# A four-stage recurrence pipeline: sums over channels as two float32r passes, and a new order of the steps

## The reference, cut to what matters

```
kk = k * k_k
kk = kk / max(sqrt(sum(kk * kk, over the 64 channels of a head)), 1e-12)
k  = k * (1 + (a - 1) * k_a)
S_t = S_{t-1} (diag(w_t) - kk_t^T (kk_t * a_t)) + v_t^T k_t ;  o_t = S_t r_t
mean = mean(o, over 64 channels);  var = mean((o - mean)^2, over 64 channels)
o = (o - mean) * rsqrt(var + 64e-5) * lnx_g + lnx_b
o = o + sum(r * k * r_k, over 64 channels) * v
o = (o * silu(g)) @ w_o
```

## Time and profile before

| | |
|---|---|
| median of three runs | 2069.64 us (2065.68 to 2069.98) |
| the profiled execution, own time | 2070.53 us |
| its span (first to last instruction) | 2068.7 us |
| mean granted TensorE clock | 0.971 of full speed |
| busy, share of the span | TensorE 92%, VectorE 49%, ScalarE 39%, GpSimd 12% |
| the recurrence in that span | about 498 to 922.5 us |

### The profile page before, as it was taken

The page is one execution under the profiler, slowest core; times in us unless marked ns, Lnnn a source line. Parts: engine busy times, 40 slices in busy tenths (PEclk is TensorE's granted clock), DMA queues, the critical chain, the costliest instruction groups (busy, mean ns, idle before and its releaser), DMA issues.

```text
span 2068.7 us, 49295 instructions
## 1 busy us (share of the span) xinstructions
PE 1906.9 (92%) x20670; PEld 1626.5 (79%) x20670; DVE 1015.3 (49%) x1655; ACT 811.9 (39%) x1422; POOL 248.7 (12%) x313
## 2 busy tenths in 40 slices
PE   7999999999999999999999989999999997787796
PEld 6988999999888888879897767777767675333696
DVE  6644364544455556524554633434454443577334
ACT  4233232334555555523333322323234443455232
POOL 0200000000343444313100000000000000000033
PEclk9999999999999999989999999999999998889898
DMA  7435555553222332124479999999999999999441
GB/s 278 170 133 181 167 173 167 168 176 127 72 86 87 97 93 70 46 77 163 146 282 353 418 419 398 425 425 425 425 413 416 424 421 370 391 378 409 158 154 61
DMA packets 128717, 508.93 MB, mean 246 GB/s; under 512 B 20257, under 2 KB 61602, under 8 KB 83234
## 3 DMA queue, kind: packets, MB, share of 16 engines
q1 hardware_dynamic: 128514, 506.01, 64.1%
HBM read 472.33 MB, written 33.63 MB: 245 GB/s over the span
## 4 chain that ended last, share of the span: by engine, by line
PE 31%; DMA 16%; DVE 3%; ACT 2%; SPq 2%; issue 2%; DVEq 0%; ACTq 0%
DMA at_vraw<-in_cache_v 16%; PE psP L2458 8%; PE psP L2460 7%; PE psP L2459 7%; PE at_psO L2508 5%; PE at_psS L2487 3%; SPq L1886 1%; PE psP L2553 0%; DVE resT L2431 0%; ACT at_p_w L2190 0%; SPq L1957 0%; DVE wlo L2232 0%; ACT at_p_w L2188 0%; PE at_psT L2499 0%; DVE at_o_new L2379 0%
## 5 line engine op out<-in xcount | busy, mean ns | idle before, releaser
L2458 PE MATMUL psP<-xhi,whi 128*128 128x320 f32 x1488 | 476.6, 320 | 6.8 <-DVE xlo L2349 3.4
L2460 PE MATMUL psP<-xhi,wlo 128*128 128x320 f32 x1488 | 461.8, 310 | 0.0
L2459 PE MATMUL psP<-xlo,whi 128*128 128x320 f32 x1488 | 461.6, 310 | 0.0
L2458 PEld LDWEIGHTS psP<-xhi,whi 128*128 128x128 f32 x1488 | 281.3, 189 | 69.7 <-issue 69.6
L2232 DVE TENSOR_TENSOR wlo<-wraw,whi 128x2048 fp32r<-128x2048 f32 x92 | 212.8, 2314 | 212.3 <-ACT whi L2070 211.9
L2070 ACT ACTIVATE whi<-wraw 128x2048 fp32r<-128x2048 f32 x92 | 175.9, 1913 | 302.0 <-PE psP L2460 300.1
L2459 PEld LDWEIGHTS psP<-xlo,whi 128*128 128x128 f32 x1488 | 281.8, 189 | 0.0
L2460 PEld LDWEIGHTS psP<-xhi,wlo 128*128 128x128 f32 x1488 | 281.4, 189 | 0.0
L131 PE MATMUL psP<-xhi,whi 128*128 128x320 f32 x704 | 218.1, 310 | 3.2 <-DVE wlo L166 2.3
L132 PE MATMUL psP<-xlo,whi 128*128 128x320 f32 x704 | 217.5, 309 | 0.0
L133 PE MATMUL psP<-xhi,wlo 128*128 128x320 f32 x704 | 217.5, 309 | 0.0
(11 more groups left out here) (344 smaller groups left out, 3228.8 us busy)
## 6 DMA issues: line engine op xcount, KB each, us to landing
wraw<-in_weights SPq DMA_DIRECT2D x160, 1024.0 KB, 6.2
at_kraw<-in_cache_k SPq DMA_DIRECT2D x96, 1024.0 KB, 11.5
at_vraw<-in_cache_v SPq DMA_DIRECT2D x96, 1024.0 KB, 10.9
at_kraw<-in_cache_k SPq DMA_DIRECT2D x64, 512.0 KB, 9.5
at_vraw<-in_cache_v SPq DMA_DIRECT2D x64, 512.0 KB, 10.1
rw_s0t<-in_s0T SPq DMA_DIRECT2D x16, 256.0 KB, 3.7
o_wkv_s<-rw_SN SPq DMA_DIRECT2D x16, 256.0 KB, 2.2
resT<-in_xT SPq DMA_DIRECT2D x4, 640.0 KB, 5.7
```

The lines of the kernel that those rows point to most:

```text
L2458: pe.matmul(out, wh, c_.xhi[:, kc, :], start=(kc == 0), stop=False)
L2459: pe.matmul(out, wh, c_.xlo[:, kc, :], start=False, stop=False)
L2460: last = pe.matmul(out, wl, c_.xhi[:, kc, :], start=False, stop=(kc == NM - 1))
```

## The change

The four sums over channels become float32r products: the operand is split into a high half and a low half, and the matrix, whose entries float32r holds exactly, is multiplied with both in one PSUM accumulation. So `over_channels` issues two float32r products in place of one float32 product.

- ss: ScalarE squares into the float32r high half `fh` (sqh), GpSimd makes the square in float32 once more (sq) and subtracts (sql, into `fl`).
- bon: ScalarE copies rk to `fh` (rkh), GpSimd subtracts (rkl).
- mean and cen: one product with the matrix "identity minus 1/64" gives the centred output in PSUM (step cen, now on TensorE). Its operand is the output of R in two halves: ScalarE copies O0 to O4 into the high half `OTh`, and VectorE has five new steps O0 to O4 that write the low half `OTl`. The VectorE step cen goes. csq and on read the centred values from PSUM.
- var: csq is split by two new VectorE steps, csqh (a copy) and csql (a subtraction).
- `ORDER` is written anew: 136 steps in place of 126.
- The temporaries sq, rk, rn, ka, fh and fl lie where the first weight chunk `wraw[:, 0]` lies. So that chunk is loaded in slot 16 (the others in slots 4, 6 and 8), the first eight ScalarE pieces are made in slot 16 in place of 15, and the first eight VectorE pieces stand at the end of slot 16 in place of all along it.

```diff
-F.a.sq F.a.ka1 R.t.U0 R.a.Q4 R.a.SA4 R.t.Q4 R.a.O0 P.t.AB R.t.SA0 R.g.Vnx R.v.U0 F.v.cs R.t.U4 P.t.s4 R.t.S0
...
+R.t.U0 R.v.U0 R.t.Q4 R.a.Q4 P.t.AB R.v.U4 R.a.SA4 R.v.SA0 P.v.D R.a.O0 R.t.U4 R.t.SA0 R.a.O4 P.t.s4 R.t.SA4
+P.v.D4s R.t.S0 R.a.SP1 F.a.kk0 F.a.sqh R.t.O0 P.a.Dt R.v.ST0 P.a.D2t R.v.O0 R.g.SAx R.v.O4 R.v.U1 P.v.FR R.a.SP2
+P.a.D2 R.v.SA1 R.t.O4 R.t.U1 P.t.Dt P.a.D4t P.v.KK R.t.SA1 R.v.SNa R.g.Vnx R.v.ST1 R.t.SN R.t.S1 P.v.s3 P.t.D2t
+P.t.D2 R.t.U2 R.v.U2 F.g.sq F.v.cs P.g.ID F.a.ka1 P.t.W R.a.O1 R.a.SP3 R.t.SA2 P.t.D4t F.a.Pi F.a.Pc F.g.sql
+F.t.ss R.a.O2 F.g.k2 R.t.S2 F.g.csm F.a.ln P.a.Vn R.t.O1 R.v.SA2 P.v.W R.v.ST2 F.g.Rz F.v.ssm P.t.Y R.t.U3 R.v.O1
+P.a.Yt P.v.Y R.t.O2 R.v.U3 R.a.O3 F.a.rkh R.v.SA3 P.a.Et P.t.Vn P.a.E R.t.SA3 R.v.O2 F.g.rkl R.a.csq F.a.rn P.t.Yt
+F.v.rk R.t.O3 P.a.E2t R.t.S3 P.t.Et P.a.E2 P.t.E R.g.SNb R.a.lnv R.t.cen R.a.rstd R.v.O3 F.a.Pm F.g.ka F.g.Kz
+P.t.Z1 P.t.E2t P.t.E2 R.v.csqh R.t.var R.v.csql P.v.Z1 P.a.E4t F.t.bon P.t.Z2 F.v.kk R.v.ST3 P.v.Z2 R.a.ong R.v.on
+P.t.E4t F.v.Az F.v.Bz P.t.Kn P.v.X P.t.Bn F.v.bonus P.t.X P.a.Bn P.a.Kn R.g.oy R.g.y R.a.xh R.v.xl""".split()
...
-            def over_channels(out, mat, x):
-                return pe.matmul(out, mat[:], x, start=True, stop=True)
+            def over_channels(out, mat, high, low):
+                pe.matmul(out, mat[:], high[:], start=True, stop=False)
+                return pe.matmul(out, mat[:], low[:], start=False, stop=True)
...
-                    elif name == "cen":
-                        R.t.wait(dve, "mean", t)
-                        R.v.done(dve.tensor_tensor(cen, OT, psR[:, banks_r.of("mean"), 0:TOK], ALU.subtract), name)
+                    elif name[0] == "O":
+                        R.a.wait(dve, name, t)
...
+                        R.v.done(dve.tensor_tensor(OTl[:, c * L:c * L + L], psR[:, banks_r.of(name), 0:L],
+                                                   OTh[:, c * L:c * L + L], ALU.subtract), name)
+                    elif name == "csqh":
...
+                        R.v.done(dve.tensor_copy(csqh[:], csq), name)
+                    elif name == "csql":
+                        R.v.wait(dve, "csqh", t)
...
+                        R.v.done(dve.tensor_tensor(csql[:], csq, csqh[:], ALU.subtract), name)
...
+                    if name == "sq":
...
+                        F.g.done(pool.tensor_tensor(sq[:], kk[:], kk[:], ALU.mult), name)
+                    elif name == "sql":
...
+                        F.g.done(pool.tensor_tensor(fl[:], sq[:], fh[:], ALU.subtract), name)
+                    elif name == "rkl":
...
+                        F.g.done(pool.tensor_tensor(fl[:], rk[:], fh[:], ALU.subtract), name)
...
+                    elif name == "rkh":
+                        F.v.wait(act, "rk", t)
+                        F.t.wait(act, "ss", t)
+                        F.a.done(act.activation(fh[:], rk[:], ACT.Copy), name)
...
-                elif slot in (4, 6, 8, 10):
-                    load_weights(slot // 2 - 2)
+                elif slot in (4, 6, 8):
+                    load_weights(slot // 2 - 1)
+                elif slot == TILES:
...
+                    load_weights(0)
...
-                elif slot == TILES - 1:
+                elif slot == TILES:
                     for q in range(2):
                         for k in range(QC):
-                            yield (QC * q + k) / 8 + 0.03
+                            yield 0.3 + 0.65 * (QC * q + k) / 8
                             split_piece(c_, act, FIRST_WO, q, k)
...
-                            yield (QC * q + k) / 8 + 0.03
+                            yield 0.97 + 0.003 * (QC * q + k)
                             low_piece(c_, dve, FIRST_WO, q, k)
```

More of the change, by code:

```diff
@@ L899, in recurrence @@
         masks, blk, blkm, I2, keep = c_.masks, c_.blk, c_.blkm, c_.I2, c_.keep
+        sq, rk, rn, ka, fh, fl = c_.front_place
         stage = c_.stage
-        OT, cen, csq, rstd = (stage[:, m] for m in range(4))
+        OT, csq, rstd = (stage[:, m] for m in range(3))
+        centre = ctx.enter_context(nc.sbuf_tensor("rw_centre", [P, P], F32R))
+        OTh, OTl, csqh, csql = (ctx.enter_context(nc.sbuf_tensor("rw_" + x, [P, TOK], F32R))
+                                for x in ("OTh", "OTl", "csqh", "csql"))
         ins = {x: sb("in_" + x, [P, TOK]) for x in ("s", "k", "a", "r", "g")}
@@ L993, in _ @@
                     F.a.wait(sp, "kk0", t)
-                    F.a.wait(sp, "sq", t)
+                    F.a.wait(sp, "sqh", t)
                     F.g.wait(sp, "k2", t)
@@ L1028, in _ @@
             pool.wait_ge(masks, c_.n_masks)
+            pool.tensor_tensor(centre[:], c_.ident[:], blkm[:], ALU.subtract).then_inc(masks, 1)
             def front(t):
@@ L1182, in run @@
                     elif name == "csq":
-                        R.v.wait(act, "cen", t)
-                        R.a.done(act.activation(csq, cen, ACT.Square), name)
+                        R.t.wait(act, "cen", t)
+                        if t:
+                            R.v.wait(act, "csql", t - 1)
+                        R.a.done(act.activation(csq, psR[:, banks_r.of("cen"), 0:TOK], ACT.Square), name)
                     elif name == "lnv":
@@ L1256, in front @@
                         loaded(dve, "r", t)
+                        if t:
+                            F.g.wait(dve, "rkl", t - 1)
                         F.v.done(dve.scalar_tensor_tensor(out=rk[:], in0=ins["r"][:], scalar=scalar("r_k", t),
@@ L1372, in beside @@
                         for k in range(QC):
-                            yield (QC * q + k) / 8 + 0.03
+                            yield 0.97 + 0.003 * (QC * q + k)
                             low_piece(c_, dve, FIRST_WO, q, k)
                 elif slot == TILES + 1:
-                    for q, step in ((2, "cen"), (3, "xl")):
+                    for q, step in ((2, "csql"), (3, "xl")):
                         for k in range(QC):
@@ L1541, in run @@
                     free_r(name, t)
-                    if name not in ("mean", "var", "SN"):
+                    if name not in ("cen", "var", "SN"):
                         ps = psR[:, banks_r.of(name)]
@@ L1584, in run @@
                         R.t.done(last, name)
-                    elif name == "mean":
+                    elif name == "cen":
+                        if t == 0:
+                            pe.wait_ge(masks, c_.n_masks + 1)
                         R.a.wait(pe, R.a.last("O0", "O1", "O2", "O3", "O4"), t)
-                        R.t.done(over_channels(psR[:, banks_r.of(name), 0:TOK], blkm, OT), name)
+                        R.v.wait(pe, R.v.last("O0", "O1", "O2", "O3", "O4"), t)
+                        R.t.done(over_channels(psR[:, banks_r.of(name), 0:TOK], centre, OTh, OTl), name)
                     elif name == "var":
-                        R.a.wait(pe, "csq", t)
-                        R.t.done(over_channels(psR[:, banks_r.of(name), 0:TOK], blkm, csq), name)
+                        R.v.wait(pe, "csqh", t)
+                        R.v.wait(pe, "csql", t)
+                        R.t.done(over_channels(psR[:, banks_r.of(name), 0:TOK], blkm, csqh, csql), name)
                     else:
@@ L1767, in combine_time, with front_place, sb @@
     return max(sample_ended(b), new_time(b, 1.0)) + 1.0
+def front_place(nc):
+    with ExitStack() as place:
+        def sb(name, dt=F32):
+            return place.enter_context(nc.sbuf_tensor("rw_" + name, [P, TOK], dt))
+        return sb("sq"), sb("rk"), sb("rn"), sb("ka"), sb("fh", F32R), sb("fl", F32R)
 def in_weights_place(nc):
```

75 lines of the change are left out of this document (48 added, 27 removed), and 3 rows, old and new, of the table READ_BY.

## The result

The changed kernel took 2122.65 us in the median of six runs (2115.57 to 2138.65), the kernel before 2069.81 us in six runs beside it (2065.68 to 2075.07): ratio 1.0267, 95% interval 1.024 to 1.0293. It is slower by 52.8 us; 2061.6 had been forecast. The profiled execution took 2119.96 us.

A forecast was written before the change was run, and what follows sets the result against it. TensorE's fixed order was taken to bound the recurrence; -15.7 + 5.3 + 1.5 + 0.3 + 0.6 = -8.0 us gave 2061.6 us in the median's terms, range 2051 to 2072.

The forecast's parts named there:

- Edits that I cost at nothing: Added ScalarE, VectorE and GpSimd work, and SyncE's loads issued later in the slot: covered by TensorE's time, cost 0.
- waits without a fixed place: TensorE's waits, 1.02 us before one slot and 0.61 us inside a group, taken as not fixed in the old order.
- TensorE's sums: Float32r pairs for ss, cen, var and bon shorten TensorE's groups: 0.98 us saved a slot, 15.7 us in 16 tiles.
- The chain from cen to var: csqh and csql on VectorE delay var, csql held by GpSimd's SNb: wait of 0.35 us in 15 slots, 5.3 us.
- Rival B: csqh is held by SNb as well, so var waits 0.85 us: 2069 us in all; chance 0.17.
- The state chain: VectorE's low half of O4 ahead of U1's copy delays SA1: 0.1 us a slot, 1.5 us in all.
- rival C: VectorE's low halves O4, O1, O2 delay the state chain by up to 1.5 us a slot: 2079 us; chance 0.10.
- Slot 16: VectorE's weight pieces at its end make TensorE wait 2.9 us in place of 2.6: +0.3 us.
- Slot 17's var: var waited 1.46 us there before; with csqh and csql about 0.6 us more.
- Rival A: The chain from cen to var is hidden, its 5.3 us not paid: -14 us, 2055.5 us; chance 0.28.

The follow-up runs named there:

- e1: Changed kernel with the load of s0t moved to the start of the slot, ahead of SyncE's waits: 2058.65 us, 0.9956 of the kernel before.
- e6: Changed kernel with s0t loaded at the slot's start, and ss and bon back to one float32 product each: 2069.27 us, 1.0008 of before.
- e7: Changed kernel with s0t loaded at the slot's start, and a third float32r pass in each of the four sums: 2070.96 us, 1.0013 of before.
- e10: Changed kernel with s0t loaded at the slot's start, SNb ahead of rkl, slot 16's ScalarE and VectorE weight pieces placed anew: 2050.02 us, 0.9914 of before.
- e5: Changed kernel with the load of s0t issued just ahead of SyncE's wait for ka, not behind it: 2058.82 us, 0.9956 of before.

## Why the prediction was wrong

**The failed step** is in "Edits that I cost at nothing": "The loads of SyncE's queue are issued later in the slot, and so are their users." That holds for k, r, a and v, whose users are the steps of the front, moved with them. It does not hold for s0t, the last of the queue, whose user Q4 is the second group of the next slot and stayed where it was. The new order has ka (which needs kk) behind csqh, csql, Z1 and kk of VectorE, and I did not ask what stood behind SyncE's wait for ka. Size: 0 forecast, 64 us measured (e1 against the changed kernel). The issue came 2.5 us nearer to the end of the slot (3.4 us ahead of its last group, now 0.9); in 14 slots that is 35 us, of the 38 by which the gaps grew, and the clock is on top with about 27.

**Its root** is "waits without a fixed place". The 1.02 us before one slot of the earlier trace rows has "ACT xhi" beside it, and I took such waits for chance. The place was fixed, Q4's start; only the length varied, with the time that the DMA took to land (2.7 to 4.6 us). A resource with no slack was already there.

**TensorE's sums** (-0.98 us a slot): right. 0.49 and 0.75 us (forecast 0.49 and 0.79) stand in the rows, and e6 and e7 price them in the whole time.

**The chain from cen to var** (+0.35): 0.39 in the row, right in size but by luck, since the parts were others. I gave csqh 0.49 us, free of SNb, and csql the hold. In fact csqh takes 0.33 free and 0.60 beside SNb, and csql, behind it, is free at 0.49. Rival B's mechanism is thus real, but its wait of 0.85 us did not come. B had csqh end 2.25 us after cen's start; it ended at 725.14 - 723.47 = 1.67. Of the difference 0.42 us is that SNb was done at 1.48 and not at 1.9: it took 1.06 us and not 1.30, and rkl ahead of it ended at 0.46 and not 0.6 (my own terms give 0.45). The other 0.16 us is that csqh ended 0.19 us behind SNb and not 0.35. The second rule of the Trainium skill (SBUF — State Buffer, Who interferes with whom) is borne out in kind: a copy within SBUF is held by a GpSimd instruction that began first. It ended 0.19 us after SNb's end (725.14 against 724.95), less than its own 0.33. In 12 of the 16 tiles of the changed kernel csqh began inside SNb; it took 0.46 to 0.60 us, and ended 0.18 to 0.19 us after SNb each time.

**The state chain** (+0.1): Dt to SA1 took 0.66 us in this slot and 0.65 to 0.76 in all but the first, against 0.58 before: a wait of 0.07 to 0.18 us. The size is right, and rival C did not come. My sum for it had 0.21 where the text names 0.23, and left out the last hop; by its own terms it gives 0.16. **Slot 16** (a wait of 2.9 us): 2.93 measured. I had assumed the clock of slot 17 as it was; it fell there before and after, for 17 and 20 us, and in e10 it did not. **Slot 17's var**: 1.07 us of wait, not 0.6 more than 1.46; small, and its cause was not tried.

**Rivals.** None was the load, so all of them, and the range with its upper end at 2072, missed. The sum with the load cured came out well: 2058.65 for 2061.6, and -6.5 us for -8.0 where the load is early in both kernels. Rival A's figure has a slip: its terms give -14.5 us, not -14.

What stays open: why some gaps of about 3 us bring the clock down and others, as the one at 731.84, do not, and what kept the clock up in slot 17 of e10.

## What to carry to other kernels

Write down, for each DMA of an in-order queue, the wait that stands ahead of it, the time to its landing and the instruction that needs it; when a step is moved, look for it among the waits of the DMA queues, and at every load behind that wait, not only at the one that it guards. If a wait always ends at one place and varies only in length, compare it with the landing of every load that the instruction reads, since a wait on several semaphores can be put down to the wrong one. A load whose buffer has long been free can go ahead of waits that guard other buffers, as s0t did in e1 and e5.

## What the runs showed of the hardware that was not expected

- A gap of some 3 us once in 24 to 28 us is dear beyond its length: about 27 of the 389.7 us of these slots were TensorE at 1.2 GHz behind it (22.5 at the least), and filling the gap with useless products made the kernel 19.6 us faster.
- In slot 17 the clock kept to its full level in e10, where the wait ahead of it was 1.0 us in place of 2.9 and the weight pieces stood elsewhere (1.00 against 0.56 over 20 us). From X to xl that was worth about 11 us with the wait itself. The length of the wait is not shown to be the cause.
- A float32 to float32r copy of 128x320 within SBUF takes VectorE 0.33 us, two thirds of a subtraction of that size (0.49). Begun while GpSimd's SNb runs, it ends 0.18 to 0.19 us after SNb does, at up to 0.60 us.
